# Block one of a two-block kernel: sums of tiles on VectorE, gates kept as tanh, a new order around the score copies

## The chip, the core and the metric

The kernel runs on one core of a Trainium2 chip: TensorE (matmuls into PSUM banks), VectorE, ScalarE, GpSimd and SyncE, which work in parallel and wait for each other by semaphores. The metric is the device time of one execution in microseconds, the median of several runs.

## The reference, cut to what matters

Two blocks of two layers each work on 256 tokens of 1024 channels, in float32. The diff touches the first block alone. One of its layers is a feed-forward stage, a token mixer with three branches, and a second feed-forward stage, each with a residual and a layer norm:

```
h = layer_norm(ALPHA * h + 0.5 * mod2 * ffn(modulate(h)))
g = sigmoid(u @ w_gates)                       # three gates of 1024 channels
merged = g0 * y_a + g1 * y_b + g2 * y_c        # convolution, state space, attention
h = layer_norm(ALPHA * h + mod5 * (merged @ w_o))
h = layer_norm(ALPHA * h + 0.5 * mod8 * ffn(modulate(h)))
```

y_b is `rms_norm(y * silu(z)) @ w_b_out` with y from sixteen state space heads; y_c is attention over compressed, selected and windowed keys, times w_c_out. layer_norm takes mean and variance over the 1024 channels of a token.

## The kernel before

Channels lie on the 128 partitions, so a tensor of 1024 channels is eight tiles of 128x256 (channels by tokens). Weights come as a stream of chunks of 128x1024 through a ring of nine places (SyncE's queue). For each chunk ScalarE rounds a high part (`high`, `later_high`, line 1226; three places), VectorE or GpSimd subtracts it from the chunk to get a low part (`low`, line 1624; `low_mix`, line 1679; GpSimd, line 2237), and TensorE multiplies high by high, high by low and low by high (`product_by_parts`, lines 485 to 496; `split_output`, line 1107). The order of work on each engine is written out by hand; each engine's instructions run in that order, and a wait holds up all that stands behind it on its engine.

A sum over channels is a sum over partitions and tiles. `accumulate_ones` (line 699) makes it on TensorE as eight f32 products with a matrix of 1/1024, one for each tile; `layer_norm` (line 706) does that for the mean, VectorE subtracts it (`centre`), ScalarE squares, and `rms` (line 711) does the same for the variance. ScalarE takes the root and VectorE its reciprocal (`inverse_root`).

Four places matter.

- End of the state space heads (heads 12 to 15 of the loops at lines 996, 1447 and 2016). TensorE makes the gates of the second branch between the heads, chunk by chunk; ScalarE copies each out of its bank (line 1461) and makes two highs behind the last one. Two copies of transposed score weights follow (line 1468), which TensorE waits for ahead of `scores(0)` (line 1125), then the squares of the last two tiles of y, then two sigmoid passes over all eight gates (line 1472), then the root (line 1475). TensorE sums the eight squares (`rms(2, m.z, 0)`, line 1130). VectorE makes the lows of two gate chunks (lines 2046 and 2047), then two pairs of maxima (line 2049), then the reciprocal, and normalizes the eight tiles of y.
- The attention loop (sixteen steps). TensorE makes the gates of the third branch into bank 1 or 2 (line 1122); ScalarE copies each out (line 1506), and one sigmoid pass over all of them stands at the loop's end (line 1536). `add_branch` on VectorE (line 1916) multiplies a branch by its gate and adds it to `merged`; `first_branch` (line 1926) starts `merged` with the first branch, whose gate keeps its sigmoid.
- Output projection (line 1177): TensorE does eight products, VectorE adds each tile to the residual (line 1659) and makes a weight low in front of it; TensorE then makes the mean (line 1185).
- End of the second feed-forward stage (lines 1733 to 1740, and 2131 and 2132): in the first layer VectorE makes three lows for the next layer, two in front of the residual and one behind it, ahead of `norm`.

Of the kernel before, what the change touches and what calls it, by code (L numbers as in the profile page):

```python
# [29 lines left out]
S = 256  # L30
D = 1024
ND = D // P
# [82 lines left out]
def gate_b(n):  # L115

    return C_SSM + 3 * (n // 2) + 2 * (n % 2)
# [125 lines left out]
class Stream:  # L243
# [25 lines left out]
    layer_done=1, par=16, umod=24, uhi=36, ulo=36, hi=6 * NF + MIX1, lo=4 * NF, lo_m=18 + SPLIT, lo_b=16, achi=2, aclo=2, ybhi=2, yblo=2, lo_g=2 * NF + FRONT_LOW,  # L269
    aside=16, back=16, whole=24, based=3, pairs=6, silu=2 * NF, hid=2 * NF, hidhi=2 * NF, hidlo=2 * NF, resid=24, mu=4, cent=32,  # L270
    sq=40, var=5, sd=5, sg=8, glu=8, copied=23, aconv=8, xconv=16, xsilu=16, kpe=2, rotp=12, rope=12,
    gelu=1, kc1=1, kcr=1, kc2=1, kcmp=1, vb=1, vbc=1, anrs=8, anorm=8, pv=8, outsg=3, gcopy=24, outm=24, dtexp=1, dtv=1,
    dtt=1, dttc=1, acs=1, acsc=1, xt=4, xdt=4, cb=4, cbm=4, bc=16, ee=16, arg=16, mm=16, yh=16, ysil=8, bnorm=8,
    cs=2, csr=2, cmx=2, cex=2, cp=2, ct=2, ptc=2, sc=16, nmx=16, ex=16, pr=16, tr=16, ptt=16, oc=4, vtt=2)
SIGNALS2 = dict(
# [17 lines left out]
def memory(nc, ctx):  # L293
# [9 lines left out]
    def tiles(a, n):  # L303
        return a.rearrange("p (n t) -> p n t", n=n)
# [103 lines left out]
    m.sq_a = m.gate_a  # L408
    m.gate_b_raw = [(kraw, sg)[n // 4][:, (n % 4) * S:(n % 4 + 1) * S] for n in range(8)]
    m.gate_b_halves = [tiles(kraw[:], 4), tiles(sg[:], 4)]  # L410
    m.gate_b = tiles(xc[:, 2048:4096], ND)
    m.gate_c = m.z
# [262 lines left out]
def tensor1(nc, t, m, sem, stream, ada, later_in):  # L675
# [4 lines left out]
    def layer(l):  # L680
# [25 lines left out]
        def layer_norm(at, src, sq, mu_bank, var_bank, resid_k):  # L706
            accumulate_ones(mu_bank, src, resid_k[0], resid_k[1], con("mean")).then_inc(sem["mu"], 1)
            rms(at[0], sq, var_bank)
            products_of_zeros(mm, m, 3 if at[0] == 0 else 8)

# [418 lines left out]
        scores(1)  # L1129
        rms(2, m.z, 0)  # L1130
        t.wait_ge(sem["ysil"], at("ysil", 4))
# [45 lines left out]
        for n in range(8):  # L1177
# [6 lines left out]
            j += 1  # L1184
        layer_norm((3,), m.h, m.u, 0, 1, ("resid", 8))


        ffn(1, C_FFN1)
        layer_norm((4,), m.h, m.u, 4, 5, ("resid", 16))

# [19 lines left out]
def scalar1(nc, a, m, sem, stream, ada, par_source, aside, con_source, con_b, next_hi, con1_source, par2_source, later_in):  # L1210
# [4 lines left out]
    def layer(l):  # L1215
# [231 lines left out]
        for h in range(16):  # L1447
            if h < 15:
                decayed(h + 1)
            if h == 0:  # L1450
                later_high(C_SSM + 2)
            if h in (2, 3):
                k = h - 2
                a.wait_ge(sem["cmx"], at("cmx", k + 1))
                act(m.pcmp[:, k, :, 0:CMP], m.pcmp[:, k, :, 0:CMP], ACT.Exp).then_inc(sem["cex"], 1)
            if h in (6, 10, 14):
                square_y(h // 2 - 3, h // 2 - 1)
            if h % 2 == 1:
                n = h // 2
                a.wait_ge(done, done_at(gate_b(n)))  # L1460
                act(m.gate_b_raw[n], ps[:, bank(s_unit + 2 + 8 * (h // 4) + (2 if n % 2 == 0 else 7 if h < 15 else 5)), 0:S],
                    ACT.Copy).then_inc(sem["gcopy"], 1)
                if n % 2 == 1:
                    later_high(gate_b(n) - 1 + HIGH)
                later_high(gate_b(n) + HIGH)
        for k in range(2):
            a.wait_ge(sem["ct"], at("ct", k + 1))
            act(m.ptc[:, 2 * k:2 * k + 2], two(ps, bank(s_unit + 32 + k)), ACT.Copy).then_inc(sem["ptc"], 1)
        square_y(6, 8)
        a.drain()  # L1470
        for k in range(2):
            last = act(m.gate_b[:, 4 * k:4 * k + 4], m.gate_b_halves[k], ACT.Sigmoid)
        last.then_inc(sem["outsg"], 1)
        a.wait_ge(sem["var"], at("var", 3))
# [29 lines left out]
        def keep_gate(n, bank_):  # L1504
            a.wait_ge(done, done_at(gate_c(n)))
            act(m.gate_c[:, n], ps[:, bank_, 0:S], ACT.Copy).then_inc(sem["gcopy"], 1)

# [26 lines left out]
        heads_out(3)  # L1534
        a.drain()
        act(m.gate_c[:], m.gate_c[:], ACT.Sigmoid).then_inc(sem["outsg"], 1)

        whole_h(1)
# [67 lines left out]
def vector1(nc, v, m, sem, stream, ada, squared, later_in, x_in, final):  # L1606
# [4 lines left out]
    def layer(l):  # L1611
# [41 lines left out]

        def residual(k0, i, place, ready, lows):
            v.wait_ge(sem["based"], at("based", i + 1))
            for n in range(ND):
                ready(n)
                lows(n)
                stt(m.h[:, n], place(n), gate(i, n), m.h[:, n], ALU.mult, ALU.add).then_inc(sem["resid"], 1)

        def centre(k, src, bank_, k0, dst=None):
# [8 lines left out]

        def norm(at, bank_, dst=None):

            centre(at[0], m.h, bank_, 0, dst)
            inverse_root(at[1], m.rs_h[:])

# [8 lines left out]
        def ffn(q, cb, keep, next_low):  # L1684
# [49 lines left out]
            def lows(n):  # L1734

                if n == 0:
                    next_low(0)
                    next_low(1)
            residual(16 * q, 2 * q, lambda n: ps[:, n // 2, (n % 2) * S:(n % 2 + 1) * S], ready, lows)
            next_low(2)  # L1740

# [7 lines left out]
        def keep_mixed():  # L1749
            v.wait_ge(ada.mixed, l + 1)  # L1750
            tt(m.mod[:, 40:48].rearrange("p (j a) -> p j a", a=2),
               ps[:, 3, 0:S].rearrange("p (a j r) -> p j a r", a=2, j=4)[:, :, :, 0],
               par("ada_b", 40, 8).rearrange("p (j a) -> p j a", a=2), ALU.add)
            v.drain()

        def mix_group(it, k, bank_):
# [159 lines left out]
        def add_branch(branch, n, y, chunk):  # L1916

            g = (m.gate_b, m.gate_c)[branch - 1][:, n]
            if n == 0:
                v.wait_ge(sem["outsg"], at("outsg", 1 + branch))  # L1920
            v.wait_ge(done, done_at(chunk))
            tt(g, y, g, ALU.mult)
            v.drain()
            tt(m.merged[:, n], m.merged[:, n], g, ALU.add).then_inc(sem["outm"], 1)  # L1924

        def first_branch(n, chunk, b):

            v.wait_ge(done, done_at(chunk))
            tt(m.merged[:, n], ps[:, b, 0:S], m.gate_a[:, n], ALU.mult).then_inc(sem["outm"], 1)

# [85 lines left out]
        for h in range(16):  # L2016
# [20 lines left out]
            if h in (5, 9, 13):  # L2037
                skip_and_gate((h - 5) // 2, (h - 5) // 2 + 2)
            if h == 1:
                low_mix(gate_b(1))  # L2040
            elif h in (2, 4, 6, 8, 10, 12):
                low_mix(gate_b(h // 2 + 1))
            elif h == 14:
                low_mix(gate_c(0))
# [76 lines left out]
        def lows(n):  # L2121
# [3 lines left out]
            elif n == 6:  # L2125
                first_low(1, 0)
        residual(8, 1, lambda n: ps[:, bank(8 + n), 0:S], lambda n: v.wait_ge(done, done_at(C_WO + n)), lows)
        centre(2, m.h, 0, 0)
        first_low(1, 1)
        inverse_root(3, m.rs_h[:])  # L2130
        ffn(1, C_FFN1, keep_last, (lambda c: first_low(2, c)) if l + 1 < DEPTH else (lambda c: None))
        norm((3, 4), 4)

# [1268 lines left out]
```

## Time and profile before

| | |
|---|---|
| median of 3 runs | 2522.7 us (2516.86 to 2528.89) |
| the profiled execution | 2523.61 us, its span 2521.6 us, mean granted TensorE clock 0.99 |
| TensorE matmuls busy | 2448.4 us, 97% |
| VectorE, ScalarE, GpSimd busy | 1872.2, 1279.5, 1077.4 us |

The span is the time between the first and the last instruction in the trace. Block one takes about the first 1770 us of it, the first layer the first 900. Times of rows are microseconds from the span's start. A busy TensorE isn't one at its peak: matmuls overlap, and their ends are modelled.

### The profile page before, as it was taken

The page shows a single profiled execution, that of the slowest core. Times are in us where ns is not written, and L with a number is a line of the kernel's source. Part 1 is how long each engine was busy: PE and PEld are TensorE (multiplying, and loading weights), DVE is VectorE, ACT ScalarE, POOL GpSimd, SP SyncE. Part 2 cuts the span into 40 slices and gives each one's busy share as a digit, 9 for nine tenths or more (in the row PEclk, how much of TensorE's full clock was granted, in tenths as well). Part 3 has the DMA queues.
Part 4 walks back from the last instruction along what each step waited for, and adds up shares of the span by engine and source line. Part 5 has one row for each costly group of instructions (what it writes and reads, how often), then busy time and mean ns, then how long its engine had stood idle before and what let it go on. Part 6 is the DMA issues. An engine that isn't in the chain of part 4 may idle for free.

```text
span 2521.6 us, 52685 instructions
## 1 busy us (share of the span) xinstructions
PE 2448.4 (97%) x20017; PEld 2309.8 (92%) x20017; DVE 1872.2 (74%) x2869; ACT 1279.5 (51%) x2099; POOL 1077.4 (43%) x618
## 2 busy tenths in 40 slices
PE   7999999999999999999999999999999999999999
PEld 4999999878989989999998788999989999989999
DVE  5875999677687687679996777776856676756776
ACT  3445456356554454444553665544654544654544
POOL 3434987312043333369871110433650344740444
PEclk9999999899999999999999999999999999999999
DMA  9885864333477677767643235875434556534564
GB/s 365 302 287 186 276 222 135 114 106 104 151 279 255 191 261 277 251 233 243 201 135 101 93 101 191 285 256 170 138 123 143 171 188 191 169 103 149 172 188 133
DMA packets 131496, 481.35 MB, mean 191 GB/s; under 512 B 14848, under 2 KB 14848, under 8 KB 130560
## 3 DMA queue, kind: packets, MB, share of 16 engines
q1 hardware_dynamic: 106992, 388.49, 47.4%
q0 software_dynamic: 23040, 83.90, 9.1%
q10 hardware_dynamic: 1296, 6.64, 0.7%
q8 instruction: 117, 1.92, 0.3%
q14 instruction: 51, 0.42, 0.1%
HBM read 475.82 MB, written 3.15 MB: 190 GB/s over the span
## 4 chain that ended last, share of the span: by engine, by line
PE 71%; DVE 16%; DVEq 5%; ACT 3%; POOL 2%; issue 2%; DMA 1%; ACTq 0%; SPq 0%; POOLq 0%
PE ps L490 12%; PE ps L492 12%; PE ps L495 11%; PE ps L547 7%; DVE ps L1837 6%; PE ps L752 3%; PE ps L758 3%; PE ps L755 3%; DVEq L1847 2%; PE ps L480 2%; PE ps L481 2%; PE ps L482 2%; PE ps L703 2%; PE ps L525 2%; POOL eb L2232 2%
## 5 line engine op out<-in xcount | busy, mean ns | idle before, releaser
L1226 ACT ACTIVATE high<-ring 128x1024 fp32r<-128x1024 f32 x493 | 518.4, 1056 | 335.3 <-PE ps L495 192.7
L492 PE MATMUL ps<-u_parts,high 128*128 128x256 f32 x3680 | 499.3, 278 | 0.0
L492 PEld LDWEIGHTS ps<-u_parts,high 128*128 128x128 f32 x3680 | 458.6, 189 | 0.0
L2183 POOL TENSOR_TENSOR ring_parts<-ring,high 128x1024 fp32r<-128x1024 f32 x88 | 227.2, 2582 | 399.0 <-ACT high L1226 398.9
L2178 POOL TENSOR_TENSOR ring_parts<-ring,high 128x1024 fp32r<-128x1024 f32 x134 | 321.8, 2420 | 79.9 <-ACT high L1226 78.3
L1624 DVE TENSOR_TENSOR ring_parts<-ring,high 128x1024 fp32r<-128x1024 f32 x176 | 216.0, 1228 | 147.9 <-ACT high L1226 135.3
L2626 ACT ACTIVATE high<-ring 128x1024 fp32r<-128x1024 f32 x227 | 239.6, 1057 | 154.3 <-PE ps L547 67.4
L3166 POOL TENSOR_TENSOR ring_parts<-ring,high 128x1024 fp32r<-128x1024 f32 x66 | 159.1, 2410 | 327.7 <-ACT high L2626 327.7
L490 PE MATMUL ps<-ac_parts,high 128*128 128x256 f32 x1824 | 246.7, 278 | 5.1 <-ACT high L1226 5.1
L495 PE MATMUL ps<-ac_parts,ring_parts 128*128 128x256 f32 x1824 | 245.6, 277 | 0.0
L490 PEld LDWEIGHTS ps<-ac_parts,high 128*128 128x128 f32 x1824 | 226.1, 188 | 5.9 <-ACT high L1226 5.9
L495 PEld LDWEIGHTS ps<-ac_parts,ring_parts 128*128 128x128 f32 x1824 | 225.1, 188 | 0.0
L3171 POOL TENSOR_TENSOR ring_parts<-ring,high 128x1024 fp32r<-128x1024 f32 x70 | 169.5, 2432 | 107.3 <-ACT high L2626 105.4
L1837 DVE SCALAR_TENSOR_TENSOR ps<-ap,par,ps 128x256 f32<-128x256 f32 x464 | 196.1, 484 | 11.5
L2237 POOL TENSOR_TENSOR ring_parts<-ring,high 128x1024 fp32r<-128x1024 f32 x32 | 76.9, 2407 | 270.8 <-ACT high L1226 270.8
L490 PE MATMUL ps<-h_parts,high 128*128 128x256 f32 x1328 | 187.8, 285 | 3.2 <-DVE ap L1924 3.2
L495 PE MATMUL ps<-h_parts,ring_parts 128*128 128x256 f32 x1328 | 180.3, 278 | 2.1 <-POOL ring_parts L2178 2.1
L3134 DVE TENSOR_TENSOR pt_parts<-pt,pt_parts 128x256 fp32r<-128x256 f32 x64 | 143.4, 2240 | 51.0 <-ACT pt_parts L2855 51.0
L490 PEld LDWEIGHTS ps<-h_parts,high 128*128 128x128 f32 x1328 | 167.8, 191 | 9.0 <-DVE ap L1924 3.6
L495 PEld LDWEIGHTS ps<-h_parts,ring_parts 128*128 128x128 f32 x1328 | 164.9, 189 | 3.3 <-POOL ring_parts L2178 3.3
L547 PE MATMUL ps<-high,pt_parts 128*128 128x256 f32 x992 | 125.5, 279 | 3.4 <-ACT pt_parts L2855 3.4
L2159 POOL DMA_DIRECT2D xc<-ada_dram x64 | 35.0, 548 | 212.0 <-DVE u L1637 160.4
(534 smaller groups left out, 4981.6 us busy)
## 6 DMA issues: line engine op xcount, KB each, us to landing
ring<-stream_dram SPq DMA_DIRECT2D x736, 512.0 KB, 3.6
xc<-ada_dram POOLq DMA_DIRECT2D x84, 512.0 KB, 5.8
z<-ada_dram POOLq DMA_DIRECT2D x36, 512.0 KB, 7.3
qr<-ada_dram POOLq DMA_DIRECT2D x36, 512.0 KB, 7.5
h_aside<-ac ACTq DMA_DIRECT2D x2, 1024.0 KB, 4.2
eb<-ada_dram POOLq DMA_DIRECT2D x4, 512.0 KB, 5.5
h<-h_aside ACTq DMA_DIRECT2D x2, 1024.0 KB, 6.9
conb<-con_dram ACTq DMA_DIRECT2D x1, 1032.0 KB, 6.6
```

Source lines behind the costliest of these rows:

```text
L490: mm(out, hi[:, k * P:(k + 1) * P], xh[:, k], start=k == 0, stop=False)
L492: mm(out, hi[:, k * P:(k + 1) * P], xl[:, k], start=False, stop=False)
L495: last = mm(out, lo[:, k * P:(k + 1) * P], xh[:, k], start=False, stop=k == ND - 1)
L547: last = mm(m.ps[:, 2 * a + quarter // 2, at], left[:, a * P:(a + 1) * P], right[:, quarter * S:(quarter + 1) * S], start=first and quarte ...
L1226: act(high_of(m, i), chunk_of(m, i), ACT.Copy).then_inc(made, 1)
L1624: tt(low_of(m, i), chunk_of(m, i), high_of(m, i), ALU.subtract).then_inc(sem["lo"], 1)
L1837: stt(sums, x, w, sums, ALU.mult, ALU.add)
L2178: nc.gpsimd.tensor_tensor(low_of(m, i), chunk_of(m, i), high_of(m, i), ALU.subtract)\
L2183: nc.gpsimd.tensor_tensor(low_of(m, i), chunk_of(m, i), high_of(m, i), ALU.subtract)\
L2626: act(high_of(m, i), chunk_of(m, i), ACT.Copy).then_inc(sem["hi"], 1)
L3166: nc.gpsimd.tensor_tensor(low_of(m, i), chunk_of(m, i), high_of(m, i), ALU.subtract)\
L3171: nc.gpsimd.tensor_tensor(low_of(m, i), chunk_of(m, i), high_of(m, i), ALU.subtract)\
```

## The change

The second and third gate are kept as tanh(x/2), made as ScalarE takes the product out of its bank; since 2 * sigmoid(x) = 1 + tanh(x/2), VectorE multiplies a branch by (tanh + 1), the first branch gets a factor 2, and the output's modulation gate is halved (`half_gate(1)`). The sigmoid passes of these two gates go, and the second gate stays where it is copied to. Behind the last state space head ScalarE does the two score copies first, then a high, the last squares, and the other high. VectorE adds the squares of the first six tiles of y into one tile, and the first seven tiles of the residual behind the output projection into one, and TensorE sums those. The second and third low for the next layer move behind the centring.

```diff
         t.wait_ge(sem["gcopy"], at("gcopy", 16))
         scores(0)
         scores(1)
-        rms(2, m.z, 0)
+        t.wait_ge(sem["ysum"], at("ysum", 1))
+        mm(ps[:, 0, 0:S], con("mean"), m.z[:, 0], start=True, stop=False)
+        for n in range(6, ND):
+            t.wait_ge(sem["sq"], at("sq", 16 + n + 1))
+            last = mm(ps[:, 0, 0:S], con("mean"), m.z[:, n], start=False, stop=n == ND - 1)
+        last.then_inc(sem["var"], 1)
...
-        layer_norm((3,), m.h, m.u, 0, 1, ("resid", 8))
+        t.wait_ge(sem["resid"], at("resid", 16))
+        mm(ps[:, 0, 0:S], con("mean"), m.rs, start=True, stop=False)
+        t.wait_ge(sem["resid"], at("resid", 17))
+        mm(ps[:, 0, 0:S], con("mean"), m.h[:, ND - 1], start=False, stop=True).then_inc(sem["mu"], 1)
+        variance(3, m.u, 1)
...
-                act(m.gate_b_raw[n], ps[:, bank(s_unit + 2 + 8 * (h // 4) + (2 if n % 2 == 0 else 7 if h < 15 else 5)), 0:S],
-                    ACT.Copy).then_inc(sem["gcopy"], 1)
-                if n % 2 == 1:
-                    later_high(gate_b(n) - 1 + HIGH)
-                later_high(gate_b(n) + HIGH)
+                act(m.gate_b[n], ps[:, bank(s_unit + 2 + 8 * (h // 4) + (2 if n % 2 == 0 else 7 if h < 15 else 5)), 0:S],
+                    ACT.Tanh, scale=0.5).then_inc(sem["gcopy"], 1)
+                if h < 15:
+                    if n % 2 == 1:
+                        later_high(gate_b(n) - 1 + HIGH)
+                    later_high(gate_b(n) + HIGH)
         for k in range(2):
             a.wait_ge(sem["ct"], at("ct", k + 1))
             act(m.ptc[:, 2 * k:2 * k + 2], two(ps, bank(s_unit + 32 + k)), ACT.Copy).then_inc(sem["ptc"], 1)
+        later_high(gate_b(7) - 1 + HIGH)
         square_y(6, 8)
-        a.drain()
-        for k in range(2):
-            last = act(m.gate_b[:, 4 * k:4 * k + 4], m.gate_b_halves[k], ACT.Sigmoid)
-        last.then_inc(sem["outsg"], 1)
+        later_high(gate_b(7) + HIGH)
...
-            act(m.gate_c[:, n], ps[:, bank_, 0:S], ACT.Copy).then_inc(sem["gcopy"], 1)
+            act(m.gate_c[:, n], ps[:, bank_, 0:S], ACT.Tanh, scale=0.5).then_inc(sem["gcopy"], 1)
...
-        a.drain()
-        act(m.gate_c[:], m.gate_c[:], ACT.Sigmoid).then_inc(sem["outsg"], 1)
-
         whole_h(1)
...
                 stt(m.h[:, n], place(n), gate(i, n), m.h[:, n], ALU.mult, ALU.add).then_inc(sem["resid"], 1)
+                if summed and 1 <= n < ND - 1:
+                    v.drain()
+                    add = tt(m.rs, m.h[:, 0] if n == 1 else m.rs, m.h[:, n], ALU.add)
+                    if n == ND - 2:
+                        add.then_inc(sem["resid"], 1)
...
             centre(at[0], m.h, bank_, 0, dst)
+            next_low(1)
+            next_low(2)
             inverse_root(at[1], m.rs_h[:])
...
                 if n == 0:
                     next_low(0)
-                    next_low(1)
...
-            next_low(2)
...
             v.drain()
+            half_gate(1)
...
-            if n == 0:
-                v.wait_ge(sem["outsg"], at("outsg", 1 + branch))
+            v.wait_ge(sem["gcopy"], at("gcopy", 8 * branch + n + 1))
             v.wait_ge(done, done_at(chunk))
-            tt(g, y, g, ALU.mult)
+            stt(g, g, 1.0, y, ALU.add, ALU.mult)
             v.drain()
             tt(m.merged[:, n], m.merged[:, n], g, ALU.add).then_inc(sem["outm"], 1)
...
-            tt(m.merged[:, n], ps[:, b, 0:S], m.gate_a[:, n], ALU.mult).then_inc(sem["outm"], 1)
+            stt(m.merged[:, n], ps[:, b, 0:S], 2.0, m.gate_a[:, n], ALU.mult, ALU.mult).then_inc(sem["outm"], 1)
...
+            if h == 15:
+                v.wait_ge(sem["sq"], at("sq", 16 + 6))
+                for n in (2, 4):
+                    tt(m.z[:, 0:2], m.z[:, 0:2], m.z[:, n:n + 2], ALU.add)
+                    v.drain()
+                tt(m.z[:, 0], m.z[:, 0], m.z[:, 1], ALU.add).then_inc(sem["ysum"], 1)
```

## Rows read from the trace of the kernel before

**Rows 1.** The page, part 1: busy time, share of the span, instructions.

```profile
PE 2448.4 (97%) x20017; PEld 2309.8 (92%) x20017; DVE 1872.2 (74%) x2869; ACT 1279.5 (51%) x2099; POOL 1077.4 (43%) x618
```

**Rows 2.** Chain of waits, 526 to 566: start, length, engine, tile, line.

```profile
542.33 1.99 ACT high L1226 x2
...
545.97 1.28 ACT L1472
...
547.26 2.00 ACT xc L1472 x2
```

**Rows 3.** Timeline, VectorE and ScalarE, 543 to 553; in brackets idle before, releaser.

```profile
543.72 0.87 DVE L1981 SCALAR_TENSOR_TENSOR xp<-xc,par,ps 128x256 f32<-128x256 f32 x2 [4.48 <-PE ps L962]
...
545.18 0.73 ACT L1444 ACTIVATE z<-xp 128x256 f32<-128x256 f32 x2
545.34 2.35 DVE L1679 TENSOR_TENSOR ring_parts<-ring,high 128x1024 fp32r<-128x1024 f32 x2
...
551.09 1.75 DVE L1668 RECIPROCAL st<-st 128x256 f32<-128x256 f32 x1 [0.64 <-ACT st L1475]
...
552.91 5.38 DVE L2086 SCALAR_TENSOR_TENSOR xp<-xp,par,st 128x256 f32<-128x256 f32 x8
```

**Rows 4.** Timeline, TensorE, 545 to 570.

```profile
545.35 1.16 PE L1060 MATMUL ps<-kr,qr 64*128 64x128 f32 x16 [1.67 <-ACT cmp L1468]
...
546.44 3.72 PE L703 MATMUL ps<-z,con 128*128 128x256 f32 x16
...
559.72 0.63 PE L1071 MATMUL ps<-con,eb 128*128 128x128 f32 x4
...
569.63 1.87 PE L490 MATMUL ps<-h_parts,high 128*128 128x256 f32 x8 [1.43 <-DVE ap L1924]
```

**Rows 5.** Windows: stretch, its length; busy PE, PEld, DVE, ACT, POOL; PEclk, DMA.

```profile
640.00:690.00 50.00, 50.00 (x386) 47.39 (x385) 31.93 (x55) 24.74 (x34) 0.00 (x0) 1.00 0.51 166
```

**Rows 6.** Chain, then VectorE's timeline, then one source line, 688 to 694.

```profile
690.29 3.47 PE ps L703 x16
...
688.65 0.48 DVE L1659 SCALAR_TENSOR_TENSOR h<-ps,mod,h 128x256 f32<-128x256 f32 x1
690.33 0.48 DVE L1659 SCALAR_TENSOR_TENSOR h<-ps,mod,h 128x256 f32<-128x256 f32 x1 [1.21 <-PE ps L482]
693.78 0.42 DVE L1664 TENSOR_TENSOR h<-h,ps 128x256 f32<-128x256 f32 x1 [2.97 <-PE ps L703]
...
L703 PE MATMUL ps<-u,con x96: 379/379/483, 226.9 to 1762.6; 128*128 128x256 f32 x96
```

**Rows 7.** Chain of waits, then ScalarE's and VectorE's timeline, 885 to 899.

```profile
885.31 2.36 DVE ring_parts L1624 x2
...
890.81 1.13 DVE ring_parts L1624
...
887.36 1.06 ACT L1226 ACTIVATE high<-ring 128x1024 fp32r<-128x1024 f32 x1 [1.66 <-PE ps L482]
...
897.07 1.75 DVE L1668 RECIPROCAL rs_h<-st 128x256 f32<-128x256 f32 x1 [2.45 <-ACT st L1298]
```

**Rows 8.** Groups by line, VectorE: busy us, mean ns of one, idle before.

```profile
L1659 DVE SCALAR_TENSOR_TENSOR h<-ps,mod,h 128x256 f32<-128x256 f32 x48 | 20.6, 477 | 7.9 <-PE ps L482 7.9
...
L1924 DVE TENSOR_TENSOR ap<-ap,xc 128x256 f32<-128x256 f32 x16 | 6.8, 426 | 1.5 <-issue 0.4
L1922 DVE TENSOR_TENSOR xc<-ps,xc 128x256 f32<-128x256 f32 x16 | 6.8, 422 | 16.8 <-PE ps L495 16.7
...
L1628 DVE TENSOR_SCALAR mod<-mod 128x8 f32<-128x8 f32 x4 | 0.7, 172 | 0.4
```

**Rows 9.** Windows around 570, and in the second layer; columns as in rows 5.

```profile
568.00:570.00 2.00, 0.57 (x6) 0.38 (x4) 1.78 (x6) 2.00 (x7) 0.00 (x0) 0.98 0.02 6
...
570.00:573.40 3.40, 3.40 (x19) 3.40 (x18) 3.33 (x7) 0.95 (x5) 0.00 (x0) 0.51 0.02 5
...
1434.00:1440.00 6.00, 5.81 (x27) 5.81 (x28) 5.35 (x16) 1.45 (x8) 0.00 (x0) 0.50 0.01 1
```

## What the change will do to the time, predicted from these rows

> **What bounds the kernel now.** I read the page first: the span, and TensorE busy in nearly all of it [rows 1]. So an edit pays only where TensorE stands still or is late, and I asked the chain of waits for the places that the diff touches. There are four, each passed once in either layer of block one.
>
> (a) The end of the state space heads, where the score copies, the last squares, the gate passes and the root lie. Here the chain runs on ScalarE, not TensorE: two highs, then (after the copies and the squares) a table load, two sigmoid passes, another load and the root, then VectorE's reciprocal [rows 2, 3]. The passes and their load are 1.28 + 2.00 = 3.3 us of it per layer, so the naive reading is that 3.3 us go. VectorE's own order says otherwise: in the same stretch it is idle only 0.64 us ahead of that reciprocal, having spent the time on two weight lows and two pairs of maxima [rows 3].
>
> (b) The attention's end and the output projection. TensorE is busy for all 50.00 of 50 us at full clock [rows 5], so the third gate's sigmoid pass, which ScalarE runs there, delays nothing that TensorE waits for.
>
> (c) The mean after the output projection. The chain lies on sixteen matmul records (eight f32 products of two passes each), 3.47 us, and VectorE waits 2.97 us for them [rows 6].
>
> (d) The end of the first layer's second feed-forward stage. The chain is VectorE's: two lows before the residual, one behind it [rows 7].
>
> **The change part by part.**
>
> *Mean after the output projection.* Eight products become two. The last residual is made at 690.33 and lasts 0.48 [rows 6]; TensorE is free at 690.29. After the change it does the product of the sums (3.47 / 8 = 0.43) while VectorE makes the last residual, and the last product starts at about 690.87 and its result is there by about 691.45 (0.43, and some 0.15 for the tail of a lone product, my estimate from the 0.38 of one record [rows 6] against its pace of 3.47 / 16 = 0.22). The centring started at 693.78. Gain 2.3 us a layer, 4.6 in all. The price is six adds of two SBUF tiles at 0.43 [rows 8], each with a drain (about 0.1), 0.5 us a tile. They fit: VectorE idles 1.21 us in front of each tile [rows 6]. The sixth add ends at about 688.65 + 0.48 + 0.1 + 0.43 = 689.7, 0.6 us ahead of need. If that cover were gone, each add would cost its 0.5 us. Bounds: 0 and 2.6 (six products) a layer.
>
> *Next layer's lows.* Two of three lows leave the space before the centring and go behind it; this happens only where a next layer exists, once. The residual then ends 1.18 us sooner (half of 2.36), and the third low (1.13) no longer stands between [rows 7]. But the mean binds next: TensorE finishes the down projection at about 887.3, where it releases ScalarE's high [rows 7], and then has eight products of 0.43, to 890.8 instead of 891.9. Gain 1.0, not 2.3. The two lows (2.36) fall into the wait for the root, which is 2.45 long [rows 7]; only 0.1 us is left, and beyond it each low costs its own length.
>
> *End of the state space heads.* In the new order ScalarE does the last gate copy, the two score copies, one high, the last two squares, then the other high, then the root; no sigmoid load, no passes. The three sums on VectorE (two over 128x512, one over 128x256; 0.7, 0.7 and 0.4, scaled from the 0.43 of a 128x256 add [rows 8], with drains 2.0) stand in the 4.48 us that VectorE idles ahead of the last heads [rows 3]. TensorE can start the scores where it now waits 1.67 us [rows 4], and the sum of squares falls from eight products to three, 3.72 x 5/8 = 2.3 us. So TensorE is some 3.4 us earlier. From the passes' end (547.26 + 2.00) to the reciprocal's start load and root take 1.83, so the root is there at about 546.9 + 1.83 = 548.7 instead of 551.1. What is late next is VectorE. The last square ends at 545.9 as before, since it waits for VectorE [rows 3]; the high behind it takes 1.0 (half of 2.00 [rows 2]) and ends at 546.9; the low that needs it ran at 546.5 and now starts at 546.95. The lows thus end 0.4 us later than 547.7, the maxima at 550.85 instead of 550.45, and the reciprocal follows at once: 550.8 against 551.09. Gain 0.3 us a layer, 0.6 in all. Bounds: 0, and the idle 0.64 a layer. The normalization behind it (5.38) and the first attention weights are VectorE's, and TensorE's first transposition at 559.72 waits for them [rows 3, 4].
>
> *Third gate.* The pass over 128x2048 goes (as many elements as the two passes of 2.00 [rows 2]), and the first wait of the branch's adds with it. TensorE is full there [rows 5], and its next need, the last merged tile, hangs on its own last product. Gain 0; up to 0.2 if that tile comes sooner.
>
> *Gates as tanh.* A copy out of the bank becomes a tanh out of the bank with a constant scale, on the same 128x256 elements: I cost it at nothing. The multiply that takes the gate, and the first branch's, change from two tensors to scalar and two tensors: 477 against 422 ns [rows 8], 0.055 x 24 a layer. Most lie under TensorE; I count 0.3 us a layer, 0.6 in all, between 0 and 2.6.
>
> *Halving the output gate.* One operation over 128x8 (0.17 [rows 8]) and a drain (0.1) on VectorE among the convolution taps, where the chain is VectorE's: +0.25 a layer, 0.5 in all.
>
> *TensorE's clock.* The granted clock falls to 1.2 GHz at 570 after TensorE was busy 0.57 of 2 us, and stays there for 3.4 us; in the second layer 6 us near 1434 run so [rows 9]. That costs half of it, 1.7 and 2.9 us, on the chain, since TensorE leads from 569.63 on [rows 4]. With TensorE 3.4 us earlier, the same work that ended at 559.7 without a gap [rows 4] ends at about 556, and TensorE then stands idle until the weights of 559.4. I expect the clock to fall there, while VectorE leads and nobody waits for a slow product, and the slow products to fill the idle stretch that now comes before 570. Whether the clock is then up at 570 is open in both layers: 0 to 4.6; I take 2.0. The Trainium skill (TensorE: Matmul & The Clock Gate, section "Part 1: The HAM clock gate") says that the throttled state is the default and activity releases it. By that rule the new idle stretch is a cost of its own, and the trace agrees as to the fall behind an idle stretch; by it alone the sum would lose these 2.0 again.
>
> Sum: -4.6 - 1.0 - 0.6 + 0.6 + 0.5 - 2.0 = -7.1 us. The profiled execution took 2523.6 us (its span 2521.6 and 2.0 around it), 0.9 above the median 2522.7: 2516.5, or 2515.6 on the median's scale. I say 2516.
>
> **The rivals.**
> *The sigmoid passes are what the chain says they are.* Then another 3.3 - 0.3 = 3.0 us a layer go, and 2510 comes out. For it: the chain [rows 2]. Against it: VectorE's 0.64 us of idle time [rows 3]. It needs VectorE to get the second low earlier than I do. Chance 0.15.
>
> *The gains are taken up.* The adds come late, or the lows behind the centring outlast the root's wait (0.1 us of room), or the clock falls in a stretch that counts. With nothing of the 2.0, half of the 4.6 and none of the 1.0, it is 2523.6 - 2.3 - 0.6 + 1.1 = 2521.8. Chance 0.14.
>
> *Tanh and Exp exchange tables.* Sixteen gate copies a layer stand between exponentials. If each needed a load before and one behind it, that is 2.57 us a copy on ScalarE; on the chain lie at least the copies ahead of the highs [rows 2], a pattern that comes three times a layer. Six such copies are 15.4 us: 2516.5 + 15.4 = 2532, and more with the attention's copies. Three pairs of loads on the chain, 7.7 us, undo the whole gain; from the fourth it is slower. For it: the kernel has no tanh, and every change to sigmoid, root or exponential shows a load. Against it: copies and squares stand between the exponentials now without one. Chance 0.04. The Trainium skill (ScalarE: Activation LUTs, section "Table sets: the hidden batching unit") lists tanh in the set whose anchor is exp; by that rule this rival falls and the sum stays. No run so far shows it.
>
> **How the numbers follow.** My forecast 0.66, full gain 0.15, taken up 0.14, tables 0.04, anything else 0.01. A measurement here tells some 0.5% (12.6 us) from no change; the three runs of before span 12 us. The likeliest case by itself reaches from 2511 (clock and bounds in its favour) to 2520. The range takes in the full gain and the taken-up gain with some of the scatter of the runs: 2507 to 2524. Faster than 2510.1: half of the full gain, a few per cent of the forecast and scatter, 0.18. Slower than 2535.3: 0.04. Within: 0.78.
>
> **What would show it.** The mean after the output projection as four records and the centring 2.3 us sooner behind the last projection. The lows of the next layer behind the centring, ending just ahead of the reciprocal. At the heads' end: no sigmoid load, the root near 548.7, yet the reciprocal no more than 0.6 us earlier, VectorE waiting for the second high; TensorE idle some 3 us ahead of the first transposition; the granted clock at 0.5 somewhere in 558 to 567. No table load at the gate copies. Wrong if the reciprocal starts by 549, if loads stand at the tanh, if the adds push the residuals, or if the clock near 570 is as low as before and other stretches are lower.

## The result: slower, outside the range

| | kernel before | changed kernel |
|---|---|---|
| median of 13 runs | 2523.93 us | 2540.24 us |
| lowest to highest | 2516.86 to 2528.89 us | 2526.63 to 2550.68 us |
| ratio, with its 95% interval | | 1.007 (1.0058 to 1.0082) |
| span of the profiled execution | 2521.6 us | 2538.5 us |

The forecast was 2516 us, with 2507 to 2524 as its range; the change costs some 16 us instead. Page, part 1, of the changed kernel, to be held against [rows 1]:

```profile
PE 2456.6 (97%) x19959; PEld 2315.8 (91%) x19973; DVE 1911.2 (75%) x2889; ACT 1267.6 (50%) x2089; POOL 1076.6 (42%) x618
```

ScalarE lost 12 us of work, as meant. VectorE gained 39 us of busy time for 20 more instructions, far more than the adds can be. The chain of waits of the changed kernel names the instruction at once (start, length, engine, tile, line). Of the longest pieces of either kernel's chain, these are the only ones of VectorE above 5 us:

```profile
260.51 10.87 DVE mod L1634
...
1132.95 10.67 DVE mod L1634
```

L1634 is `half_gate`, one scaling over 128x8 in SBUF, which [rows 8] show at 172 ns. VectorE's timeline there, and GpSimd's in the same stretch:

```profile
259.94 0.41 DVE L1806 TENSOR_TENSOR ap<-ps,sg 128x256 f32<-128x256 f32 x1
260.28 0.15 DVE L1762 TENSOR_TENSOR mod<-ps,par 128x8 f32<-128x8 f32 x1
260.51 10.87 DVE L1634 TENSOR_SCALAR mod<-mod 128x8 f32<-128x8 f32 x1
271.52 0.88 DVE L1849 SCALAR_TENSOR_TENSOR ps<-ap,par,ps 128x256 f32<-128x256 f32 x2
```

```profile
254.80 21.45 POOL L2196 TENSOR_TENSOR ring_parts<-ring,high 128x1024 fp32r<-128x1024 f32 x9
```

The reader is to see three things. The sum just ahead of the halving (L1762) has the same shape and takes 0.15 us; one of its two operands lies in PSUM. The taps around it work on sums in PSUM and run at their pace (two in 0.88 us). And GpSimd runs nine weight lows end to end, 21.45 / 9 = 2.38 us each, and shows no idle time during the whole 10.87 us. So the theory to test (A): a VectorE operation that has only SBUF on its sides is kept out while GpSimd works on SBUF, and it isn't let in between two lows if the second is ready. The rivals: the time is lost by another part of the change (B); the stall belongs to the instruction, the wait or the drain at this place, whatever the operands (C).

The other steps, in the same trace. Head end, first layer: VectorE, then ScalarE (as [rows 3]):

```profile
557.09 0.87 DVE L1992 SCALAR_TENSOR_TENSOR xp<-xc,par,ps 128x256 f32<-128x256 f32 x2 [2.62 <-PE ps L963]
...
560.23 1.23 DVE L1692 TENSOR_TENSOR ring_parts<-ring,high 128x1024 fp32r<-128x1024 f32 x1 [0.29 <-ACT high L1236]
...
564.12 1.74 DVE L1679 RECIPROCAL st<-st 128x256 f32<-128x256 f32 x1
```

```profile
558.50 0.75 ACT L1454 ACTIVATE z<-xp 128x256 f32<-128x256 f32 x2 [0.61 <-DVE xp L1995]
559.15 1.04 ACT L1236 ACTIVATE high<-ring 128x1024 fp32r<-128x1024 f32 x1
560.21 1.28 ACT L1484 ACT_TABLE_LOAD   x1
561.51 0.47 ACT L1484 ACTIVATE st<-ps,con 128x256 f32<-128x256 f32 x1
```

Mean after the output projection, on VectorE (as [rows 6]):

```profile
700.97 0.48 DVE L1665 SCALAR_TENSOR_TENSOR h<-ps,mod,h 128x256 f32<-128x256 f32 x1 [0.58 <-PE ps L480]
702.25 2.73 DVE L1675 TENSOR_TENSOR h<-h,ps 128x256 f32<-128x256 f32 x8 [0.79 <-PE ps L1194]
```

End of the first layer's second feed-forward stage, ScalarE and VectorE (as [rows 7]):

```profile
897.17 1.06 ACT L1236 ACTIVATE high<-ring 128x1024 fp32r<-128x1024 f32 x1 [1.66 <-PE ps L480]
...
903.22 2.35 DVE L1630 TENSOR_TENSOR ring_parts<-ring,high 128x1024 fp32r<-128x1024 f32 x2
905.75 1.75 DVE L1679 RECIPROCAL rs_h<-st 128x256 f32<-128x256 f32 x1 [0.18 <-ACT st L1308]
```

All three came out close to the forecast, as told point by point below.

### The profile page after: what moved, and what is told of

The parts are those of the page before. It is cut to its first block, busy times and chain, and to the rows that moved or that the text cites. A ratio compares the mean times of both kernels' runs of the same rounds, so it can differ in the third digit from the quotient of the medians.

```text
span 2538.5 us, 52635 instructions
## 1 busy us (share of the span) xinstructions
PE 2456.6 (97%) x19959; PEld 2315.8 (91%) x19973; DVE 1911.2 (75%) x2889; ACT 1267.6 (50%) x2089; POOL 1076.6 (42%) x618
## 3 DMA queue, kind: packets, MB, share of 16 engines
HBM read 475.82 MB, written 3.15 MB: 189 GB/s over the span
## 4 chain that ended last, share of the span: by engine, by line
PE 76%; DVE 12%; DVEq 4%; ACT 2%; POOL 2%; issue 2%; DMA 1%; ACTq 0%; POOLq 0%
PE ps L488 14%; PE ps L490 13%; PE ps L493 13%; PE ps L545 7%; DVE ps L1849 4%; PE ps L753 3%; PE ps L756 3%; PE ps L759 3%; PE ps L701 2%; PE ps L478 2%; PE ps L480 2%; PE ps L479 2%; POOL eb L2250 2%; DVEq L1859 1%; PE ps L523 1%
## 5 line engine op out<-in xcount | busy, mean ns | idle before, releaser
L545 PEld LDWEIGHTS ps<-high,pt_parts 128*128 128x128 f32 x992 | 119.7, 188 | 3.7 <-ACT high L2644 3.7
```

The costliest lines, as they stand in the source:

```text
L545: last = mm(m.ps[:, 2 * a + quarter // 2, at], left[:, a * P:(a + 1) * P], right[:, quarter * S:(quarter + 1) * S], start=first and quarte ...
```

## The experiments

Eight kernels; the first four have one set of runs of the kernel before beside them (median 2520.63 us), the last four another (2520.11). Times are medians; ratios are against the kernel before, with 95% intervals.

| run | median us | ratio (interval) | the 128x8 operation in round 13, layers 0 and 1 |
|---|---|---|---|
| gate_in_heads | 2510.46 | 0.9958 (0.9944 to 0.9972) | not there; 0.17 in the heads |
| gate_from_psum | 2511.62 | 0.9961 (0.9947 to 0.9976) | 0.17, 0.17 |
| before_plus_scale | 2550.60 | 1.0115 (1.0100 to 1.0129) | 15.58, 15.58 |
| lows_drained | 2567.17 | 1.0185 (1.0171 to 1.0200) | 0.17, 1.12 |
| two_forms | 2524.39, one run | | 15.58, 0.17 |
| low_waits | 2516.26 | 0.9983 (0.9972 to 0.9994) | 1.47, 1.47 |
| mean_undone | 2516.99 | 0.9987 (0.9975 to 0.9998) | not there |
| highs_first | 2512.50 | 0.9970 (0.9955 to 0.9984) | not there |

**gate_in_heads: the halving moved.**

```diff
             v.drain()
-            half_gate(1)
...
             elif h == 3:
+                half_gate(1)
                 affine(nc, v, m, 2, par("ln_g", 8, 8), par("ln_b", 8, 8))
```

> The changed kernel with the halving of the output gate moved from round 13 of the convolution into the state space heads, beside the entry of the second FFN. Theory A (the halving reads and writes SBUF only and is kept out while GpSimd's lows follow one another without a gap, 10.87 and 10.67 us in the two layers, plus some 3 us of what that makes late): the halving takes 0.17 us, the convolution ends as in the kernel before, and the time is 2514 to 2520 us, 4 to 10 us under the kernel before. Rival B (the time went elsewhere, for example to the copies as tanh or to the squares that come later): the time stays above 2530 us. Rival C (the stall is a matter of the instruction and not of the place): some 10 us are lost at the new place.

Measured 2510.46 us, some 10 us under the kernel before and under the expected 2514 to 2520. The line of the halving, all six executions (ns, least, median, most):

```profile
L1634 DVE TENSOR_SCALAR mod<-mod x6: 160/171/172, 214.5 to 1731.0; 128x8 f32<-128x8 f32 x6
```

Rivals B and C fall: the same instruction at another place, where GpSimd does nothing, costs 0.17, and the rest of the change is a gain. This version beats both kernels.

**gate_from_psum: same place, other operand.**

```diff
-            tt(m.mod[:, 40:48].rearrange(...), ...
+            tt(ps[:, 3, S:S + 8].rearrange(...), ...
             v.drain()
-            half_gate(1)
+            ts(m.mod[:, 40:48], ps[:, 3, S:S + 8], 0.5, None, ALU.mult)
+            v.drain()
```

> The changed kernel with the halving left in round 13, but the sum of the gate's row and its bias is written into PSUM and the halving reads it there; the wait, the drains and the count of instructions are the same. Theory A: an operation with its input in PSUM isn't kept out by GpSimd, so the halving takes about 0.2 us, and the time is that of the kernel with the halving moved, within 2 us: 2514 to 2520 us. Rival C (the place, the drain or the wait costs the time, whatever the operands): still 10 to 11 us for the halving or its drain, and 2538 to 2543 us.

```profile
L1766 DVE TENSOR_SCALAR mod<-ps x2: 166/166/167, 262.2 to 1120.5; 128x8 f32<-128x8 f32 x2
```

The same wait, drains, place and count, a GpSimd low under way in both layers, and 0.17 us. It is the operand's memory that decides. The time is within 2 us of gate_in_heads, as expected, and like it under 2514 to 2520.

**before_plus_scale: this part alone.** The kernel before with `ts(g, g, 1.0, None, ALU.mult)` over the gate's columns and a drain, behind the sum in round 13; the result is unchanged.

> The kernel before, with one instruction and its drain added: the output gate's eight columns are multiplied by 1.0 in round 13, in SBUF, in both layers. Theory A: the instruction takes 10 to 11 us in each layer and the time is 20 to 26 us over the kernel before, 2544 to 2550 us. Rival B (the loss belongs to other parts of the change): 2523 to 2526 us.

Measured 30 us over the kernel before, more than expected, because each instance took 15.58 us. Rival B falls here too. GpSimd's timeline, then VectorE's:

```profile
254.64 21.25 POOL L2181 TENSOR_TENSOR ring_parts<-ring,high 128x1024 fp32r<-128x1024 f32 x9
276.04 4.89 POOL L2181 TENSOR_TENSOR ring_parts<-ring,high 128x1024 fp32r<-128x1024 f32 x2 [0.15 <-ACT high L1226]
```

```profile
260.35 15.58 DVE L1756 TENSOR_SCALAR mod<-mod 128x8 f32<-128x8 f32 x1
```

The length differs because the end of the wait differs. The scaling was done at 260.35 + 15.58 = 275.93: right after GpSimd's ninth low (254.64 + 21.25 = 275.89) and ahead of the tenth, the first for which GpSimd had to wait (0.15 us, for a high). In the changed kernel the halving was done at 271.38, between GpSimd's seventh low and its eighth, and there GpSimd did not stand still. What the eighth low has in common with that tenth is a late high. In each pair, the high and the low that needs it; first the changed kernel's eighth low, then the ninth of before_plus_scale, which did not let the scaling in:

```profile
270.10 1.05 ACT L1236 ACTIVATE high<-ring 128x1024 fp32r<-128x1024 f32 x1
271.32 2.40 POOL L2196 TENSOR_TENSOR ring_parts<-ring,high 128x1024 fp32r<-128x1024 f32 x1
```

```profile
271.97 1.06 ACT L1226 ACTIVATE high<-ring 128x1024 fp32r<-128x1024 f32 x1 [1.45 <-PE ps L495]
273.50 2.38 POOL L2181 TENSOR_TENSOR ring_parts<-ring,high 128x1024 fp32r<-128x1024 f32 x1
```

The first high ended 0.17 us ahead of its low, the second 0.47. So the operation isn't let in at the next end of a low, but at the first low that was ready only just in time, or not in time; where between 0.17 and 0.47 us the limit lies, these runs don't show.

**lows_drained: gaps by drains.** `g.drain()` behind each of GpSimd's lows in the mixers, the halving where the change has it.

> The changed kernel with the halving where the change has it, and a drain on GpSimd behind each of its lows in the mixers, so that the next low is not begun while the one before runs. Theory A1 (GpSimd's next low, ready ahead, takes the port over without a gap, and VectorE gets in only at a gap): the halving takes at most one low, 2.4 us or less, and the time falls to some 2516 to 2526 us, less what the drains cost GpSimd. Theory A2 (a drain makes no gap that counts): the halving still takes 10 to 11 us and the time stays above 2535 us.

The halving fell to 1.12 us at most, as A1 says, but the time rose to 2567 us instead of falling. The waits of 232 to 420 say what the drains cost (us in total, times, longest); the second row was 7.4 us, 4 times, in the changed kernel:

```profile
POOL ring_parts L2196 <- issue: 18.1, 36, 2.4
...
PE ps L493 <- POOL ring_parts L2196: 21.0, 17, 5.7
```

GpSimd was late for TensorE, and its lows no longer followed one another anyway. So it doesn't settle what a drain does for the halving; low_waits leaves the drains out.

**low_waits: one gap.** The halving signals, and GpSimd waits for it ahead of one low.

```diff
+            last = ts(g, g, 0.5, None, ALU.mult)
+            if i == 1:
+                last.then_inc(sem["halved"], 1)
...
         for n, i in enumerate(range(C_MIX, C_CK)):
+            if n == 10:
+                g.wait_ge(sem["halved"], at("halved", 1))
             low(i)
```

> The changed kernel with the halving where the change has it, and one wait added on GpSimd: its eleventh low of the mixer (the one that began at 261.88, behind the low under way as the halving began) waits until the halving is done. Theory A1 (the low under way holds the halving, and the next one, if it is ready, follows without letting it in): the halving takes what is left of the low under way, 0.5 to 2.4 us, in both layers, GpSimd begins that low right behind it, and the time is 2512 to 2519 us. Rival (the halving waits for something else that ends at 271.4, so that GpSimd now waits with it): 10 to 11 us as before for both, and 2540 us or more.

VectorE's timeline, then GpSimd's:

```profile
261.87 1.47 DVE L1634 TENSOR_SCALAR mod<-mod 128x8 f32<-128x8 f32 x1
...
1123.15 1.47 DVE L1634 TENSOR_SCALAR mod<-mod 128x8 f32<-128x8 f32 x1
```

```profile
260.89 2.41 POOL L2198 TENSOR_TENSOR ring_parts<-ring,high 128x1024 fp32r<-128x1024 f32 x1
263.42 2.40 POOL L2198 TENSOR_TENSOR ring_parts<-ring,high 128x1024 fp32r<-128x1024 f32 x1
```

The halving ends at 263.34, with the low begun at 260.89 (its end is 263.30), and the next begins at 263.42. With the next low kept back, the price is the rest of the low under way, and the time is within the expected 2512 to 2519 us. Still, it is less good than the halving elsewhere (0.9983 against 0.9958).

**two_forms: which operands.** gate_in_heads, and in round 13 one operation without use: layer 0 `tt(m.sc1[:, 8:16], g, g, ALU.add)`, layer 1 `ts(ps[:, 3, S:S + 8], g, 0.5, None, ALU.mult)`, each with a drain.

> The changed kernel with the halving moved to the heads, and one instruction added in round 13 whose result nobody uses: in layer 0 a sum of two operands that both lie in SBUF, in layer 1 a scaling that reads SBUF and writes PSUM; both over 128x8, with a drain. Theory A, by the pattern that operations of both kinds showed elsewhere: the sum with two operands in SBUF is kept out like the scaling was, 10 to 16 us until GpSimd next waits for a high; the scaling that writes PSUM takes 0.2 us. Rival C (only the scaling in place, SBUF to SBUF, is kept out): 0.2 us for both. Rival D (any read of SBUF is kept out): 10 to 16 us for both.

```profile
L1768 DVE TENSOR_TENSOR sc<-mod x1: 15581/15581/15581, 260.7 to 260.7; 128x8 f32<-128x8 f32 x1
...
L1770 DVE TENSOR_SCALAR ps<-mod x1: 170/170/170, 1133.4 to 1133.4; 128x8 f32<-128x8 f32 x1
```

Rivals C and D fall, each on one execution of one profile; GpSimd had a low under way at both. A sum of two operands in SBUF is kept out like the scaling in place; one read from SBUF with the result in PSUM is not.

**mean_undone: the largest gain by itself.** gate_in_heads, with the mean behind the output projection as eight products over h again and no running sums on VectorE.

> The changed kernel with the halving moved to the heads and the mean behind the output projection as before the change: eight products over h behind the last residual, no sums on VectorE. By the working of the prediction this gives back 2.3 us in each layer between the last residual and the reciprocal, 4.6 in all: 2513 to 2517 us. Rival (the gain of that stretch is the clock's alone, ahead of it): no change, 2510 to 2511 us.

From the end of the last residual to the reciprocal's start it is 8.16 us in both layers, the same as in the kernel before, against 5.99 with the change: 2.17 a layer. The time, 2516.99 us, is as expected. It rose by 6.5 us, or 0.0029 in the ratio; with intervals of some 0.0013 to either side of both ratios that is 3 to 12 us, and the 4.3 read from the traces lie within it.

**highs_first: the order on ScalarE.**

```diff
-                if h < 15:
-                    if n % 2 == 1:
-                        later_high(gate_b(n) - 1 + HIGH)
-                    later_high(gate_b(n) + HIGH)
+                if n % 2 == 1:
+                    later_high(gate_b(n) - 1 + HIGH)
+                later_high(gate_b(n) + HIGH)
...
-        later_high(gate_b(7) - 1 + HIGH)
         square_y(6, 8)
-        later_high(gate_b(7) + HIGH)
```

> The changed kernel with the halving moved to the heads, and on ScalarE the last two highs of the heads back in their old place, behind the copy of the last gate and ahead of the score copies and the last squares; no pass of sigmoid comes back. By the order on ScalarE the last squares end 0.5 to 1 us later, and so does the root: 0.3 to 1 us a layer up to the reciprocal, 2511 to 2513 us. Rival (the order of the highs is what sets when TensorE falls idle and when its clock falls, so that the slow products come back behind the heads): 2 us a layer, 2514 to 2516 us.

The time lies in the expected 2511 to 2513 us, but by luck, for the working behind it missed. From VectorE's last heads to the reciprocal it is 6.65 us in both layers, 0.38 less than in gate_in_heads (7.03) and not 0.3 to 1 more: VectorE no longer waits 0.3 us for the second high, and the root, done at 547.96, is still ahead of VectorE. But the clock moved. Windows (stretch, length; busy PE, PEld, DVE, ACT, POOL; PEclk, DMA share), gate_in_heads, whose reciprocal starts at 553.18:

```profile
560.00:562.00 2.00, 0.19 (x2) 0.22 (x3) 1.85 (x8) 1.58 (x5) 0.00 (x0) 1.00 0.67 242
562.00:564.00 2.00, 1.52 (x10) 1.10 (x10) 2.00 (x3) 2.00 (x9) 0.00 (x0) 0.62 0.02 8
...
566.00:568.00 2.00, 2.00 (x11) 2.00 (x11) 1.86 (x3) 1.80 (x8) 0.52 (x1) 0.50 0.00 0
568.00:570.00 2.00, 2.00 (x14) 2.00 (x13) 1.92 (x6) 0.00 (x0) 0.00 (x0) 0.67 0.00 0
570.00:572.00 2.00, 1.39 (x14) 1.03 (x13) 1.79 (x5) 1.54 (x3) 0.00 (x0) 1.00 0.40 94
```

and highs_first, whose reciprocal starts at 549.80:

```profile
562.00:564.00 2.00, 1.87 (x16) 1.66 (x15) 2.00 (x2) 1.51 (x7) 1.17 (x1) 1.00 0.00 0
564.00:566.00 2.00, 0.41 (x4) 0.42 (x4) 1.85 (x8) 0.43 (x2) 0.00 (x0) 1.00 0.49 115
...
568.00:570.00 2.00, 1.68 (x8) 1.68 (x9) 1.85 (x8) 1.65 (x8) 0.00 (x0) 0.59 0.00 0
570.00:572.00 2.00, 2.00 (x12) 2.00 (x12) 1.93 (x3) 0.00 (x0) 0.00 (x0) 0.56 0.00 0
```

In gate_in_heads TensorE stands still 3.01 us ahead of the first attention weights, and the clock falls some 9 us behind the reciprocal, for 7 us. In highs_first it stands still for 1.44 us there, the clock stays up, and it falls 19 us behind the reciprocal, where it also fell in the kernel before [rows 9]. From this reciprocal to that behind the output projection it is 143.12 us in gate_in_heads and 146.27 in highs_first, in the first layer. So what the rival says came in the first layer, with 3.15 us. In the second layer of highs_first the clock was down for 3 us in the early place, with 144.73 us against 144.83. The times of the two kernels (2510.46, 2512.50) can't be told apart.

## Why the prediction was wrong

**The step that failed** is "Halving the output gate": 0.17 and a drain 0.1, "+0.25 a layer, 0.5 in all". It measured 10.87 and 10.67 us, 21.5 in all. I took the mean of a group whose four executions each fall in a pause of GpSimd of 5.76 us, 0.6 to 0.8 us before its next low, and asked only whether VectorE leads the chain there, not who else uses SBUF. The kernel before had a row that warns, one line in two of its forms, which the prediction doesn't use (ns, least, median, most):

```profile
L1599 DVE TENSOR_TENSOR entry<-par,sc x4: 166/168/169, 212.6 to 1361.4; 128x8 f32<-128x8 f32 x4
L1599 DVE TENSOR_TENSOR entry<-ln_last,sc x3: 168/2337/2344, 31.0 to 1745.3; 128x8 f32<-128x8 f32 x3
```

The same 128x8 product of two SBUF tiles, 0.17 us or 2.34; the last of the slow ones begins at 1745.27, beside a low of GpSimd from 1745.19 on that lasts 2.40. A group whose most is fourteen times its least is two cases, and the reader is to ask which of them the new instruction will be. The normalization of [rows 3] holds such a case too (same columns):

```profile
L2086 DVE SCALAR_TENSOR_TENSOR xp<-xp,par,st x16: 471/480/2601, 552.9 to 1422.0; 128x256 f32<-128x256 f32 x16
```

Of its eight tiles in the first layer seven take 0.48 us and one, from 555.30 on, 2.60, beside a GpSimd low from 555.17 on that lasts 2.45. The prediction counts all 5.38 us as VectorE's work; some 2.1 of them are this wait, ahead of the first attention weights.

The Trainium skill (SBUF — State Buffer, section "Who interferes with whom") says that VectorE and GpSimd share a pair of SBUF ports under an exclusive lock, that a scaling within SBUF can take it, that an operation with two SBUF inputs contends with a GpSimd operation that reads SBUF, and that the one that comes second blocks until the other is done. The kinds of operands agree with two_forms and gate_from_psum. The length doesn't: taken by that rule, an estimate of the cost is at most one low, 2.4 us a layer. The runs show 10.67 to 15.58, because a low that is ready well ahead follows without letting VectorE in; the measurement decides.

**More was lost than the stalls.** From the reciprocal behind the first feed-forward stage to that in the heads the changed kernel takes 333.64 us and gate_in_heads 319.45 in the first layer, 332.12 and 317.91 in the second: 14.2 more in each, 3.3 and 3.5 above the stalls themselves. Two more reciprocals divide that stretch into three. Up to the first, the convolution and what follows it, the loss is the stall and 0.3 us (190.62 against 179.39, and 190.28 against 179.36). The second part loses 1.5 and 1.6 (35.87 against 34.39, and 36.09 against 34.47), the third 1.5 and 1.7 (107.15 against 105.67, and 105.75 against 104.08).

The third part's loss goes with TensorE's clock and needs no stall: the part is longer where the clock is down for longer in it. The first 43 us of it, in the first layer of the changed kernel (107.15 us long) and of gate_in_heads (105.67), and in the second layer of two_forms, where nothing was kept out (107.31); columns as in [rows 5]:

```profile
457.00:500.00 43.00, 41.43 (x312) 38.56 (x311) 27.05 (x51) 15.77 (x25) 15.62 (x13) 0.80 0.35 106
```

```profile
447.50:490.50 43.00, 41.43 (x326) 38.63 (x325) 28.07 (x55) 16.70 (x25) 15.74 (x13) 0.84 0.37 115
```

```profile
1317.50:1360.50 43.00, 41.43 (x312) 38.62 (x311) 26.96 (x51) 15.74 (x25) 15.68 (x13) 0.80 0.32 105
```

The granted clock is 0.80, 0.84 and 0.80 there. The layer of two_forms with a stall of 15.58 us has 0.88 and 103.92 us. Why the second part lost 1.5 us stays open: two_forms has 35.83 us in the layer with the stall and 34.09 in the other, but before_plus_scale, with the same stall, 34.24, and over the three parts it lost 15.5 on the kernel before (335.45 against 319.96), so nothing beyond the stall.

**Mean after the output projection: right.** Forecast 2.3 us a layer; from the last residual's start to the centring it was 3.45 [rows 6] and is 1.28, so 2.17, and mean_undone gives back just this. The adds were hidden.

**Next layer's lows: right.** From the high that the down projection releases to the reciprocal it was 9.71 [rows 7] and is 8.58: 1.13, forecast 1.0. The two moved lows end at 905.57, in time: the reciprocal at 905.75 waits for the root. The whole stage took 198.10 and 198.06 us in the two kernels without the move and 196.95 to 196.99 in seven of the eight with it; the eighth, the changed kernel itself, took 198.32, one of two lengths that such stages have (last section).

**End of the state space heads: right.** 7.37 [rows 3] became 7.03 in both layers, 0.34 against 0.3. VectorE bounds it, waiting 0.29 for the second high, as forecast; the 3.3 us of sigmoid passes were not there to be had, so that rival fell. highs_first shows that 0.72 a layer were, with the highs left where they stood.

**Gates as tanh: right as to the tables.** No load stands at the tanh copies, and one takes 376 ns in the median (375 to 376 as a copy before). The Trainium skill (ScalarE: Activation LUTs, section "Table sets: the hidden batching unit") puts tanh with exp, and the trace agrees. The multiplies were mis-sized: forecast 0.6 us in all for 477 against 422 ns, but in the changed kernel they take what the old ones took (422 [rows 8] and 418):

```profile
L1933 DVE SCALAR_TENSOR_TENSOR z<-z,ps x16: 410/420/422, 665.8 to 1551.9; 128x256 f32<-128x256 f32 x16
L1940 DVE SCALAR_TENSOR_TENSOR ap<-ps,pt x16: 410/414/425, 480.3 to 1422.9; 128x256 f32<-128x256 f32 x16
```

**TensorE's clock: right in kind.** The 3.01 us of idle time came, the clock fell there, and where it did so for 7 us, it was up at the later place. In gate_in_heads that held in both layers; in the changed kernel in the first only, and the later fall came as well in the second. With the 2.17 of the mean taken off, the stretch from reciprocal to reciprocal fell from 147.88 to 143.12 and from 149.91 to 144.83, so 2.6 and 2.9 us are left, 5.5 in all; forecast was 2.0 for both layers, with 4.6 as the most. These are single profiles: the six kernels with both the new order and the new mean have 143.12 to 145.01 us in the first layer and 143.24 to 146.38 in the second, which leaves 0.7 to 2.6 and 1.4 to 4.5. How much of it is the clock's, and how much the third gate's pass, isn't separated. The time at the lower clock did not shrink: the mean granted clock of the stretch was 0.99 and 0.98 before and is 0.98 in both layers of gate_in_heads. It moved to where less waits for TensorE.

**The sum without its wrong term** is -7.6 us, or -8.2 with the multiplies at nothing; gate_in_heads gives -10 with an interval of -7 to -14. The slower outcome came by a mechanism that no rival named.

## What to carry to other kernels

Before a small operation is added to VectorE, look at what GpSimd does in that stretch: if GpSimd works on SBUF without a gap, give the operation an operand in PSUM, or put it where GpSimd is idle. Read the least and the most of a group, not its mean: two levels in one group mean two conditions. An instruction's size says nothing of its price when it has to wait for GpSimd, and this wait shows as busy time, not as idle time.

## What the runs showed of the hardware

- The stall has no bound in the operation itself: 128x8 elements waited 10.67 to 15.58 us, through lows of 2.4 us each. It ended at a low whose high had come 0.17 us ahead (changed kernel), for which GpSimd had to wait (before_plus_scale, two_forms), or that was held back (low_waits); lows that followed one another, without a drain, and whose highs had come 0.45 us ahead or more let nothing in. It counts as VectorE's busy time.
- Reading PSUM (0.166 us, gate_from_psum) or writing PSUM (0.170 us, two_forms) spared the operation the wait, with a low under way.
- An idle stretch of 3.0 to 3.1 us on TensorE ahead of the first attention weights brought the clock to 1.2 GHz there in both layers of all seven kernels that had it (the changed one, gate_in_heads, gate_from_psum, lows_drained, two_forms, low_waits, mean_undone), for 3 to 7 us. Where it was down for 6 us or more (11 layers) it didn't fall again at the later place; where for 3 to 4 (3 layers), it did.
- Feed-forward stages took about 196.95 or about 198.3 us from reciprocal to reciprocal, at full granted clock, also where no edit touches them: the first stage of the second layer took 198.32 in the kernel before and 196.92 in before_plus_scale, 196.95 in gate_in_heads and 198.32 in gate_from_psum. A single profile can't settle 1.4 us on such a stage.
